# One block for the output projection and the MLP, block ends without the GpSimd queue drain, and an eviction moved from VectorE to ScalarE

## The reference

```python
mix = jnp.concatenate(blocks, axis=1)                      # both attention groups
x = x + g1 * jnp.einsum('bsm,md->bsd', mix, w_out[l])      # output projection
h2 = rmsnorm(x, norm2_g[l]) * (1.0 + sc2) + sh2
ff = jnp.einsum('bsf,fd->bsd',
                jnp.square(jax.nn.relu(jnp.einsum('bsd,df->bsf', h2, w_ff1[l]))), w_ff2[l])
x = x + g2 * ff
return rmsnorm(x, final_g)
```

## Time and profile before

| what | value |
|---|---|
| median of 3 runs | 3772.91 us (3772.84 to 3782.22) |
| the profiled execution, its own time | 3766.84 us |
| its span | 3764.7 us |
| PE busy, share of the span | 3256.0 us, 86% |
| DVE | 2533.4 us, 67% |
| ACT | 1838.7 us, 49% |
| POOL | 371.4 us, 10% |
| mean granted PE clock | 0.931 of full speed |

### The profile page before, as it was taken

One profiled execution on the slowest core, in us unless ns is written; L12 is line 12 of the kernel. 1 busy time (PEld: TensorE's weight loads), 2 busy tenths in 40 slices (PEclk: granted clock), 3 DMA queues, 4 the chain that ended last, 5 costly groups with the idle time before them and its releaser, 6 DMA issues. The chain is left out here.

```text
span 3764.7 us, 44996 instructions
## 1 busy us (share of the span) xinstructions
PE 3256.0 (86%) x15808; PEld 2612.6 (69%) x15808; DVE 2533.4 (67%) x4792; ACT 1838.7 (49%) x3059; POOL 371.4 (10%) x587
## 2 busy tenths in 40 slices
PE   3797877899795798977789969959989999999998
PEld 2675666777674576765667748748868887888887
DVE  5542688877891677676776637677788775565676
ACT  2310577878672788878866743232232222322232
POOL 0010011110100100000000000002211220000131
PEclk7898999999896899989899989979999999999999
DMA  6354332322335432111111025455454445664565
GB/s 208 107 194 125 107 105 90 97 88 69 102 98 157 138 101 68 46 48 31 40 33 36 18 104 162 140 175 175 154 179 143 154 146 207 229 223 157 193 219 191
DMA packets 334617, 475.95 MB, mean 126 GB/s; under 512 B 29056, under 2 KB 218704, under 8 KB 333984
## 3 DMA queue, kind: packets, MB, share of 16 engines
q1 hardware_dynamic: 285936, 308.29, 26.0%
q0 software_dynamic: 48464, 164.88, 12.4%
HBM read 316.07 MB, written 156.98 MB: 126 GB/s over the span
## 5 line engine op out<-in xcount | busy, mean ns | idle before, releaser
L2034 PE MATMUL m_ps<-m_h,w_hi 128*128 128x512 f32 x1792 | 559.8, 394 | 55.4 <-DVE w_lo L1761 19.0
L2034 PEld LDWEIGHTS m_ps<-m_h,w_hi 128*128 128x128 f32 x1792 | 340.3, 190 | 130.3 <-issue 34.4
L904 DVE SCALAR_TENSOR_TENSOR rank<-spare,iw,rank 128x1024 f32<-128x1024 f32 (+5 forms) x330 | 332.0, 1021 | 72.0 <-ACT spare L833 67.3
L2045 PE MATMUL m_ps<-w_hi,a_hi 128*128 128x512 f32 x896 | 350.6, 391 | 12.0 <-DVE w_lo L1917 8.9
L2034 PE MATMUL m_ps<-m_h,w_lo 128*128 128x512 f32 x896 | 352.2, 393 | 0.0
L2045 PE MATMUL m_ps<-w_lo,a_hi 128*128 128x512 f32 x896 | 350.3, 391 | 0.0
L2045 PE MATMUL m_ps<-w_hi,a_lo 128*128 128x512 f32 x896 | 350.0, 391 | 0.0
L833 ACT ACTIVATE spare<-isps 128x1024 f32<-128x1024 f32 (+5 forms) x352 | 280.1, 813 | 119.7 <-PE isps L801 87.1
L801 PE MATMUL isps<-ki,iq_hi 128*128 128x512 f32 (+3 forms) x608 | 238.8, 394 | 90.7 <-ACT spare L833 67.1
L2588 ACT ACTIVATE pt<-tps 128x512 f32<-128x512 f32 (+1 forms) x432 | 233.4, 573 | 109.1 <-PE tps L2527 52.3
L2527 PE MATMUL tps<-ident,probs 128*128 128x128 f32 x1632 | 239.1, 287 | 45.0 <-DVE probs L2743 27.4
(11 more groups left out here) (281 smaller groups left out, 7045.0 us busy)
## 6 DMA issues: line engine op xcount, KB each, us to landing
w_raw<-in_w_ff SPq DMA_DIRECT2D x136, 512.0 KB, 5.4
dram_aop<-a_out POOLq DMA_DIRECT2D x224, 256.0 KB, 2.6
a_lo<-dram_aop SPq DMA_DIRECT2D x56, 1024.0 KB, 5.8
ada_w<-in_w_ada POOLq DMA_DIRECT2D x16, 1024.0 KB, 8.6
q_hi<-dram_proj_hi SPq DMA_DIRECT2D x128, 128.0 KB, 3.0
q_lo<-dram_proj_lo SPq DMA_DIRECT2D x128, 128.0 KB, 3.0
iq_hi<-dram_proj_hi SPq DMA_DIRECT2D x224, 64.0 KB, 2.4
iq_lo<-dram_proj_lo SPq DMA_DIRECT2D x224, 64.0 KB, 2.5
```

The lines of the kernel that those rows point to most:

```text
L904: nc.vector.scalar_tensor_tensor(out=dst, in0=got, scalar=w, in1=dst, op0=ALU.mult, op1=ALU.add).then_inc(s_acc, 1)
L2034: mm = nc.tensor.matmul(ps[:, b], w[:, m % WOPS, k, :], hop[:, j, h, :, k, :], start=fresh and k == 0 and i == 0, stop=k == KH - 1 and i == 2,
L2045: mm = nc.tensor.matmul(ps[:, t], a[:, c % RING, k, t * P:(t + 1) * P], w[:, c % RING, k, :], start=first and i == 0, stop=last and i == 2 ...
```

## The change

Three edits.

- `output` and `mlp` become one block, `output_mlp`. The MLP's buffers lie over buffers of the output stage, so waits stand where there was a barrier. Loads and splits of the MLP's first part are put into the last steps of the output pipeline by `early(t)`; `product(0, 0)` runs on PE ahead of the last `step` but one, and `h_low(0, P_A11)` stands in DVE's step 16 between `x1` and the variance.
- The eviction of `hps` into `h2` moves from the head of DVE's step to the middle of ACT's step.

```diff
-        with nc.Block() as block:
+        with nc.Block(no_gpsimd_drain=True) as block:
...
 (ACT's step)
                         nc.scalar.activation(oss[:, 2:3], oss[:, 1:2], ACT.Sqrt).then_inc(s_std, 1)
+                    if there(t - 2):
+                        act.wait_ge(s_ht, t - 1)
+                        if there(t - 2, 2):
+                            act.wait_ge(s_so[slot], (t - 2 - slot) * 8)
+                        for k in range(KT):
+                            last = nc.scalar.activation(h2[:, slot, k, :], hps[:, k * P:(k + 1) * P], ACT.Identity,
+                                                        scale=keep.cols[:, 2, k:k + 1], bias=keep.cols[:, 3, k:k + 1])
+                        last.then_inc(s_hu, 1)
                     if there(t + 2):
                         act.wait_ge(s_hs, t + 3)
...
 (DVE's step)
-                    if there(t - 2):
-
-                        dve.wait_ge(s_ht, t - 1)
-                        if there(t - 2, 2):
-                            dve.wait_ge(s_so[slot], (t - 2 - slot) * 8)
-                        for k in range(KT):
-                            last = nc.vector.tensor_scalar(h2[:, slot, k, :], hps[:, k * P:(k + 1) * P],
-                                                           keep.cols[:, 2, k:k + 1], keep.cols[:, 3, k:k + 1],
-                                                           ALU.mult, ALU.add)
-                        last.then_inc(s_hu, 1)
...
                     if there(t - 1):
+                        if isinstance(t, int) and t == NB:
+                            h_low(0, P_A11)
                         dve.wait_ge(s_ss, t)
...
 (SP, ahead of step(t) for t = 12 to 17)
+                def early(t):
+                    if t == 12:
+                        sp.wait_ge(s_wl, KT)
+                        load_w1(0)
+                        load_slot(0, P_A11, 0, 0)
+                    if t == 13:
+                        load_sums(0)
+                    if t == 14:
+                        load_w1(1)
+                        sp.dma_start(g2[:], bc(scr.gates[1])).then_inc(q_g, 16)
+                    if t == NB:
+                        sp.wait_ge(s_o, NB)
+                        load_slot(0, P_S2, 0, 0)
+                        load_slot(0, P_A12, 0, 1)
+                        load_slot(0, P_S4, 0, 1)
+
+                steps(sp, step, early=early)
                 for slot in range(2):
                     sp.wait_ge(s_xo[slot], 16 * (NB // 2))
-                    sp.wait_ge(s_so[slot], 16 * (NB // 2))
+                load_slot(0, P_A22, 1, 1)
...
 (ACT)
+                def early(t):
+                    if t == 13:
+                        w1_hi(0, 0)
+                    if t == 14:
+                        w1_hi(0, 1)
+                        w1_hi(0, 2)
+                    if t == 15:
+                        w1_hi(0, 3)
+                    if t == NB:
+                        h_hi(0, P_A11)
+
+                steps(act, step, weights, early)
+                h_hi(0, P_S1)
+                h_hi(0, P_S2)
+                h_hi(0, P_A12)
+                h_hi(0, P_S3)
+                h_hi(0, P_S4)
+                h_hi(0, P_A22)
...
 (DVE)
+                def early(t):
+                    if t == 13:
+                        w1_sums12(0)
+                        w1_low(0, 0)
+                    if t == 14:
+                        w1_low(0, 1)
+                        w1_low(0, 2)
+                    if t == 15:
+                        w1_low(0, 3)
+                        w1_sum3(0)
+                        sum_s1(0)
+
+                steps(dve, step, weights, early)
+                h_low(0, P_S1)
+                sum_s3(0)
+                sum_s2(0)
+                h_low(0, P_S2)
+                h_low(0, P_A12)
+                h_low(0, P_S3)
+                sum_s4(0)
+                h_low(0, P_S4)
+                h_low(0, P_A22)
...
 (PE)
+                def early(t):
+                    if t == NB:
+                        product(0, 0)
+
+                steps(pe, step, early=early)
                 for n in range(NS):
                     for j in range(7):
-                        product(n, j)
+                        if n or j:
+                            product(n, j)
```

More of the change, by code:

```diff
@@ L1411, in mlp, with there, steps @@
         q_o = sem("s_out_stored3")
+        def there(tile, least=0):
+            return not isinstance(tile, int) or least <= tile < NB
+        def steps(eng, step, weights=None, early=None):
+            for t in range(FIRST, LOOP):
+                if t == 0 and weights is not None:
+                    weights()
+                step(t, t % 2)
+            with eng.Fori(LOOP // 2, LOOP_END // 2) as pair:
+                for slot in range(2):
+                    step(pair * 2 + slot, slot)
+            for t in range(LOOP_END, LAST + 1):
+                if early is not None:
+                    early(t)
+                step(t, t % 2)
         def h_lo(j):
-            return hop[:, j, 1]
+            return hop[:, j, 0]
         def w1_part(n, j):
@@ L1875, in _, with w2_step @@
                     w1_sum3(n + 1)
-                step = [0]
-                def then(ins):
-                    step[0] += 1
+                count = [0]
+                def w2_step(ins):
+                    count[0] += 1
                     ins.then_inc(c_ts, 1)
-                    dve.wait_ge(c_ts, step[0])
+                    dve.wait_ge(c_ts, count[0])
                 def w2_sum(c):
@@ L2008, in _, with step @@
             def _(pe):
+                def step(t, slot):
+                    other = 1 - slot
+                    if there(t + 1):
+                        pe.wait_ge(s_m, t + 2)
+                        if there(t):
+                            pe.wait_ge(s_ml, t + 1)
+                        for k in range(KT):
+                            tr = nc.tensor.transpose(mps[:, k * P:(k + 1) * P], mix[:, other, k * P:(k + 1) * P],
+                                                     keep.ident[:])
+                        tr.then_inc(s_mt, 1)
+                    if there(t):
+                        pe.wait_ge(s_ml, t + 1)
+                        if there(t, 2):
+                            pe.wait_ge(s_x1, t - 1)
+                        for half in range(2):
+                            n = 0
+                            for k in range(KT):
+                                if isinstance(t, int) and t == 0:
+                                    pe.wait_ge(s_wl, k + 1)
+                                for a, b in ((mt_hi, wo_hi), (mt_hi, wo_lo), (mt_lo, wo_hi)):
+                                    mm = nc.tensor.matmul(ops[:, slot, half * 512:(half + 1) * 512], a[:, slot, k, :],
+                                                          b[:, k, half * 512:(half + 1) * 512],
+                                                          start=n == 0, stop=n == 3 * KT - 1)
+                                    n += 1
+                        mm.then_inc(s_o, 1)
+                    if there(t - 1):
+                        pe.wait_ge(s_xn, t)
+                        if there(t - 2):
+                            pe.wait_ge(s_hu, t - 1)
+                        for k in range(KT):
+                            tr = nc.tensor.transpose(hps[:, k * P:(k + 1) * P], xn[:, k * P:(k + 1) * P], keep.ident[:])
+                        tr.then_inc(s_ht, 1)
                 low_at = {P_A11: 1, P_S2: 3, P_A12: 4, P_S1: 4, P_S3: 5, P_S4: 6, P_A22: 7}
```

483 lines of the change are left out of this document (209 added, 274 removed).

## The result

The changed kernel takes **3748.87 us** (median of 4 runs, 3740.3 to 3750.56) against 3777.56 us for the kernel before in the same comparison (4 runs, 3772.84 to 3782.5). The ratio is 0.9919, 95% interval 0.9896 to 0.9943: about 0.8% faster. The medians are 28.7 us apart, the sum of the prediction was 27.1, and 3745.8 was forecast in 3732 to 3758.

A forecast was written before the change was run, and what follows sets the result against it. PE was taken as the bound, busy 86% of the span and pacing the output loop at 12.94 us a tile. 18.6 + 22.2 - 13.7 = 27.1 us off the 3772.91 us median gave 3745.8 us, range 3732 to 3758.

The forecast's parts named there:

- Block ends: POOL's exposed drains at the ends of indexing, attention and the kernel come free: 4.95 + 8.88 + 4.78 = 18.6 us.
- Rival C: At the kernel's end, the last drain is paid outside the span: 3750.6 us; chance 0.22.
- The eviction: Output loop: eight ACT instructions behind the root lengthen the chain to 14.08 us against PE's 12.94; 13.7 us lost.
- Rival B: Output loop: the eviction is hidden on ACT, with no loss, giving 3732.1 us; chance 0.12.
- A gain is excluded by PE's pace: Output loop: PE sets 12.94 us a tile, so moving the eviction off DVE can gain nothing.
- The merged start: Last output matmul (T) to product(0, 2): 37.6 us instead of 59.8, because sums and splits start earlier; 22.2 us gained.
- Rival D: MLP start: sums find loads late or DVE's list holds something back; gain 12, not 22, so 3756 us; chance 0.11.
- E: Output stage: PE's waits put it to its low clock; 12 tiles cost 103 us, giving 3849 us; chance 0.03.
- F: Output stage: ACT loads a table twice per tile, costing 30.8 us, giving 3776.6 us; chance 0.03.
- The sum and the reference: Whole kernel: 27.1 us saved, taken from the 3772.91 us median rather than the profiled execution's 3766.84, giving 3745.8.

The follow-up runs named there:

- flags_only: The kernel before with only no_gpsimd_drain=True added on its six blocks; 3752.73 us against 3772.93, ratio 0.9951.
- evict_act_only: The kernel before with only the h2 eviction moved from DVE to ACT, behind the root; 3783.28 us against 3772.93, ratio 1.0034.
- after_evict_early: The changed kernel with the eviction still on ACT but right behind mt_hi, ahead of the square of x1; 3729.46 us, ratio 0.9889 to the kernel before.
- early_split: after_evict_early with h_hi(0, P_S1) moved ahead of ACT's last step; 3719.7 us against 3769.96 for the kernel before, ratio 0.9868.
- mt_32_bytes: The kernel before with only mt_hi and mt_lo moved by 32 bytes in each partition; 3771.74 us against a single 3772.95, a single run.

## Why the prediction was right, point by point

- **Block ends: right in mechanism and size.** 18.6 predicted, 5.0 + 8.6 + 4.85 = 18.45 in the profiles, 20.2 as a run of its own by the medians, with 18.3 at the three ends of its profile. Each exposed drain was worth its entry. Rival C, that the last one is paid outside the span, fell: 2.1 us lie outside in flags_only and 1.8 in the changed kernel.
- **The eviction: right, with one premise wrong beneath it.** Predicted 14.08 us a step, an instruction of 459 ns, a loss of 13.7; measured 14.05, 467 and 13.3, and in evict_act_only 14.05 again. Rival B (hidden) fell with PE's wait of 1.1 us in each step. The Trainium skill, page "ScalarE: Activation LUTs", section "Rules for kernel authors", wants multiply and add on VectorE. For the changed kernel the runs agree (1.4 us a step), but after_evict_early shows the limit: on ScalarE at another place in its list they cost nothing. By the Trainium skill, the same page, section "What ACT_TABLE_LOAD costs", eight were to take 3.09 us (an estimate by that page); the trace has 2.74, and the measurement decides.
- **"A gain is excluded by PE's pace": this step failed.** I took 12.94 us a step for a property of the 48 matmuls and 16 transposes. With the buffers of the merged block the same work takes 12.65 to 12.69. This did not show in the time, because ACT's chain of 14.05 lay over it; it hid a gain of about 4 us and made the eviction's real cost in the merged kernel 12 x (14.05 - 12.65) = 16.8 us instead of 13.3. In the changed kernel the missed gain and the missed cost cancel. That the forecast did not suffer from this is luck, and only undoing the eviction brought it to light.
- **The merged start: right, 0.8 us too much.** 22.2 predicted, 21.4 measured. `product(0, 0)` started at T + 4.8 as predicted but held PE for 5.2 us, where I had 4.3, so the split of S1 came 0.7 us later; the chain behind it took 24.56 for 24.5. The cause is the clock: I had put its matmuls partly at the low level, and the granted clock was 0.51 through all of it. In early_split it was 0.67 over the same product, which took 4.1 us. Rival D (late loads) fell: no such wait.
- **E and F fell.** The granted clock in the loop is 1.00 with PE waiting in each step, and the output stage has one table load.
- **Not foreseen:** from the barrier to the first transposes of `mix` it takes 11.7 us instead of 12.9, 1.2 less. No edit need be the cause: in six profiles with the drains kept this stretch takes 11.85 to 12.9 us, in the six without them 11.5 to 12.2. The output stages of before and after differ by 11.1 and not by the 13.3 of the twelve steps because of this and because the other steps and the last tile are 0.9 us shorter together.
- **The sum and the reference.** The three predicted terms measure 18.45 + 21.4 - 13.3 = 26.55 us where 27.1 were predicted. That is the agreement which the profiles show. The 28.7 of the medians is no finer test, since its interval reaches from 21.5 to 39.3 us. The profiled pair is only 17.6 apart, because its untouched stages ran 11.1 us longer. Why they did is open.

## What to carry to other kernels

Work moved to an idle engine is priced by its place in that engine's list, not by the engine's idle share: find the chain through the loop, measure its slack, and put the moved instructions where the engine waits for that chain anyway. An exposed drain is worth its own entry if what ended last before it is still last without it. When an edit also moves buffers, compare the pace of the bound engine itself, since one effect can lie hidden beneath another.

## What the runs showed of the hardware

- The start address of a matmul's weight operand in SBUF can change PE's pace: 0.2333 us between matmuls of 128 x 512 in the three profiles with the old place (before, flags_only, evict_act_only), 0.227 in the profiles with it moved, by 32 bytes (mt_32_bytes) or more, all at full granted clock. The rule behind it is open.
- An ACTIVATE on 128x128 out of PSUM with scale and bias as per-partition operands takes 467 ns in the changed kernel. Eight in a row take 2.74 us to the start of the next instruction, 0.34 each, so neighbours overlap by 0.12 us; with one such operand it was 0.10.
- The drain of POOL at the end of a block takes 4.78 to 8.95 us in the kernel before, and 0.05 us at the ends of `values` and `output`, where POOL issues no DMA. With `no_gpsimd_drain=True` the barrier follows POOL's last wait within 0.2 us.
